# Attention queries of token tiles 2 and 3 made after the first head's scores, and three early heads instead of four

## The chip, the cores and the metric

The kernel runs on one core of a Trainium2 chip. Its engines work side by side, each through its own queue in program order: TensorE (PE, matrix products; PEld is its loading of weights), VectorE (DVE), ScalarE (ACT), GpSimdE (POOL) and SyncE (SP, which only issues transfers). They meet through semaphores. DMA engines move data between the chip's memory and the core's local memory. The metric is the device time of one execution in microseconds.

## The reference

One step of one decoder layer, for 512 prompt tokens and 32 sample tokens (8 sequences of 4), D = 1024, all in float32:

```
n = RMSNorm(h)
[u | conv input | q (4 heads x 128) | gates (3 x 1024)] = n @ w_in + b_in
branch A: S5 state space scan on u, GLU, projection
branch B: GLU, causal depthwise convolution (31 taps), LayerNorm, swish, projection
branch C: cross-attention of q into 256 memory tokens (4 heads), projection
h = h + (sum of sigmoid(gate_b) * branch_b) @ w_out
h = h + PEER(RMSNorm(h))
y = RMSNorm(h)
```

PEER, for each token: 8 heads; a head's query (256 wide) is scored against 2 x 128 keys, the best 16 of each half are combined and the best 16 of the 256 sums name 16 of 16384 experts. For each of the 128 experts chosen, a row u and a row v (1024 each) are fetched from a table: gelu(u . x) times the softmax of the scores weighs v, and the weighted rows are added to h.

## The kernel before

The tokens are cut into tiles of 128: tiles 0 and 1 are the first half (FIRST = 256 columns), tiles 2 and 3 and the 32 sample tokens (tile 4) the rest. The program has two parts.

**The trunk of the first half.** TensorE makes, in the order of the list JOBS, keys and values of the memory, the inputs of the three branches, the scan's products, the attention of tiles 0 and 1 and of the samples, gates and projections for 256 columns, and the output product (jobs o0 to o7). Each job is written into one of four pairs of PSUM banks, a pair is reused four jobs later, and weights come through a ring of six places of 512 KB (`load`). The attention queries are jobs q0 to q3: each is made by `weighted` for all 544 columns, as two halves of 272 columns over 8 slices of weights. In the profile a float32 product is two instructions, so a query is 32 of them; ScalarE adds the bias and writes qT.

**The experts.** An expert step n is one tile and one head; there are 34 steps (EXPERTS), and 16 rows each, so 544 rows. For each row POOL issues an indirect DMA that fetches u and v for 128 tokens (1 MB) into a ring of 10 places (RING). DVE takes the dot product with u, ScalarE applies gelu to four dots together, DVE multiplies by the softmax gate (`weigh`), and for three rows of four ScalarE builds a diagonal matrix with which TensorE adds the weighted v (line 1157); the fourth is added by DVE. Only then is the row's ring place free and POOL can fetch the row that is 10 later.

Between the two parts stands the routing. PEER queries of head 0 (Aq0) are made between the jobs o5 to o7; then TensorE runs the scores of head 0 (As0, line 1000), transposes of h (ht, L1006) and of the normalised input (xt, L1011), the queries of heads 1 and 2, the scores of head 1, and so on up to the scores of head EARLY_HEADS - 1. Queries and scores use four single PSUM banks in the order of BANK_JOBS. DVE routes head 0 (`route_first`; its indices let POOL fetch rows 0 to 15), then head 1 (`route(1)`), and after that begins with the dots; later routes are cut into pieces that run between dots. What is left, that is the heads from EARLY_HEADS on and the whole trunk of the second half (its attention, gates, projections, output product, norm, routing scores), is woven by `rest_of_trunk` into the expert rows: after each row TensorE takes 2 or 5 matrix products of it (`late_matmuls`). PLACE gives for each piece the row at which it falls, from its count in BANK_JOBS; ScalarE and DVE do their parts of it a few rows later. The weights of all this come through four places of 512 KB: `late_load` m waits until the product that used load m - 4 is done.

ScalarE's queue between the parts is: head 0's scores, h and x copies, then per early head the queries, the scores and, after some of them, the exponential of a routed head (`exp_of`), and only then gelu of the first dots.

Of the kernel before, what the change touches and what calls it, by code (L numbers as in the profile page):

```python
# [52 lines left out]
DIAGS = 8  # L53
LAG = 2
GROUP = 4
EARLY_HEADS = 4


COLS, _at = {}, 0
# [29 lines left out]

BANK_JOBS = [("As0.0", 0), ("Aq1.0", 0), ("As0.1", 0), ("Aq1.1", 0)]
for _h in range(1, PH):
    _late = int(_h >= EARLY_HEADS)
    if _h + 1 < PH:
# [107 lines left out]
def hybrid_step(nc, a, o):  # L203
    ctx = ExitStack()
    with ctx:
        def sem(name):
            return ctx.enter_context(nc.semaphore(name))
# [10 lines left out]
        def at(start, *shape):  # L218
            n = 1
            for x in shape:  # L220
                n *= x
            piece, first = (arenas[0], 0) if start < SPLIT_AT else (arenas[1], SPLIT_AT)
            v = piece[:, start - first:start - first + n]
            names = "abcd"[:len(shape)]
            if len(shape) > 1:
                v = v.rearrange(f"p ({' '.join(names)}) -> p {' '.join(names)}",
                                **{x: s for x, s in zip(names[1:], shape[1:])})
            return v
# [73 lines left out]
        h2sq = at(30976, KD, FIRST)  # L302
        xbT = at(44728, KD, FIRST)
        late_w = at(0, 4, 1024)
        qbuf = at(4096, 2, 2, RQ)
        gsg_b = at(22912, 2, 3, REST)
        merged_b = at(44728, KD, REST)
# [54 lines left out]
        def c(name, i=0, n=1):  # L362
# [37 lines left out]
        bank_full = [sem(f"bank_full{i}") for i in range(4)]  # L400
        bank_free = [sem(f"bank_free{i}") for i in range(4)]
        late_in = [sem(f"late_w_in{i}") for i in range(4)]
        x2b_in, mergeb_ok, h2sqb_ok, h2rb_ok, xbTb_ok = (sem(n) for n in (
            "x2b_in", "mergeb_ok", "h2sqb_ok", "h2rb_ok", "xbTb_ok"))

# [5 lines left out]
        def filled(eng, name):  # L411

            p, n = JOB[name]
            eng.wait_ge(full[p], n + 1)
            return pairs[p]
# [52 lines left out]
        def _(sp):  # L468
# [59 lines left out]
            def late_load(name, src, k=KD):  # L528
# [7 lines left out]
                    bank_filled(sp, BANK_LOADS[m - 4])  # L536
                sp.dma_start(late_w[:, m % 4, 0:k * P], src).then_inc(late_in[m % 4], 16)

            for h in range(PH):
                for b in range(2):  # L540
                    late_load(f"Aq{h}.{b}", a["peer_q"][2 * h + b])
# [27 lines left out]
        def _(pool):  # L569
# [58 lines left out]
            for g in range(TOPK * NJ):  # L628
                n, j = g // TOPK, g % TOPK
                if g == 0:  # L630
                    pool.wait_ge(half_routed, 1)
                elif g == 8:
                    pool.wait_ge(routed, 1)
                elif j == 0:
                    pool.wait_ge(routed, n + 1)
                if g == 6:
                    for t in range(2):
                        filled(pool, f"ht{t}")
                if g >= RING:
                    by, count = V_USERS[g - RING]  # L640
                    pool.wait_ge(v_used[by], count)
                    pool.sem_inc(slot_free, 1)
                pool.indirect_dma_start(row(g), None, a["peer_uv"],  # L643
                                        bass.IndirectOffsetOnAxis(ap=idx[:, n % 8, j:j + 1], axis=0)
                                        ).then_inc(row_in[g % RING], 16)
# [3 lines left out]
        def _(pe):  # L649
# [116 lines left out]
                mm.then_inc(full[JOB[f"z1{h}"][0]], 1)  # L766
            weighted("ai3", nT)
            for j in range(4):
                weighted(f"q{j}", nT)
            gates(0, 1)  # L770

            for n in ("q0", "q1", "q2", "q3", "k0", "k1", "k2", "k3", "v"):
# [230 lines left out]
            for t in range(2):  # L1003
                ps = flat(begin(f"ht{t}"), 1024)
                for k in range(KD):
                    mm = pe.transpose(ps[:, k * P:(k + 1) * P], h2T[:, k, t * P:(t + 1) * P], ident)  # L1006
                mm.then_inc(full[JOB[f"ht{t}"][0]], 1)
            for t in range(2):
                ps = flat(begin(f"xt{t}"), 1024)
                for k in range(KD):  # L1010
                    mm = pe.transpose(ps[:, k * P:(k + 1) * P], xbT[:, k, t * P:(t + 1) * P], ident)  # L1011
                mm.then_inc(full[JOB[f"xt{t}"][0]], 1)
            pe.wait_ge(rcol_ok, 1)
            for _ in first_queries(1):
                pass
            for _ in first_heads(1, EARLY_HEADS):
# [23 lines left out]
            def late_attention(t, stage):  # L1040

                for b in range(2):
                    name = f"b{stage}{t}.{b}"
                    ps = begin_bank(name)
                    if stage == "a":
                        pe.wait_ge(kv_copied, 48)
                    elif stage == "t":
                        pe.wait_ge(bp_ok, 2 * (t - 2) + b + 1)
                    else:
                        bank_emptied(pe, f"bt{t}.{b}")  # L1050
                    share = shares_b(b)
                    for h in range(2):
                        if stage == "a":
                            mm = pe.matmul(ps[:, MEM * h:MEM * (h + 1)], qT[:, 2 * b + h, t * P:(t + 1) * P],
                                           kT_b[:, 2 * b + h, :], start=True, stop=True)
                            if h == 1:
                                mm.then_inc(bank_full[BANK[name][0]], 1)
                            yield
                            continue
                        for m in range(2):  # L1060
                            part = share[:, h, P * m:P * (m + 1)]
                            if stage == "t":
                                n = 2 * h + m
                                mm = pe.transpose(ps[:, P * n:P * (n + 1)], part, ident)
                            else:
                                mm = pe.matmul(ps[:, P * h:P * (h + 1)], values_b(m, 2 * b + h), part,
                                               start=(m == 0), stop=(m == 1))
                            if h == 1 and m == 1:
                                mm.then_inc(bank_full[BANK[name][0]], 1)
                            yield  # L1070
# [95 lines left out]
        def _(act):  # L1166
# [86 lines left out]
            glu_input(3)  # L1253
            for j in range(4):
                ps = filled(act, f"q{j}")
                act.activation(halves(qT[:, j, :]), two(ps), ACT.Identity, bias=c("b_in", 12 + j)
                               ).then_inc(drained(f"q{j}"), 1)
            act.wait_ge(q_zero, 1)
            for j in range(4):
# [138 lines left out]
            for t in range(2):  # L1398
                ps = filled(act, f"ht{t}")
                act.wait_ge(kv_copied, 48)  # L1400
                act.activation(h2(t), flat(ps, 1024), ACT.Copy).then_inc(drained(f"ht{t}"), 1)
            for t in range(2):
                ps = filled(act, f"xt{t}")
                act.activation(xb(t), flat(ps, 1024), ACT.Copy).then_inc(drained(f"xt{t}"), 1)
            first_query(1)
            for h in range(1, EARLY_HEADS):
                first_query(h + 1)
                if h == 1:
                    act.wait_ge(rcol_ok, 3)
                first_score(h)  # L1410
                if h != 2:
                    exp_of(h // 2)

            def late_exps(t, b):

# [931 lines left out]
```

## Time and profile before

| | us |
|---|---|
| median of 3 runs | 1943.35 (1941.68 to 1944.21) |
| profiled execution | 1947.41 |
| its span, first to last instruction | 1945.6 |
| PE / DVE / ACT / POOL busy | 1674.4 / 1388.4 / 521.7 / 663.9 |
| mean granted TensorE clock | 0.949 |

Durations below are of the profiled execution, in microseconds from the start of its span unless marked otherwise. A granted clock of 1.00 is 2.4 GHz and 0.50 is 1.2 GHz. DMA share is the mean busy share of the 16 DMA engines. A line number is that of the code or of a helper. An entry in square brackets gives the engine's idle time before the instruction and what ended it.

### The profile page before, as it was taken

The numbers are of one execution on the slowest core, as the hardware profiler recorded it, in microseconds if no ns is written. First come the engines' busy times: TensorE is split into PE (matmuls) and PEld (weight loads), VectorE is DVE, ScalarE is ACT, GpSimd is POOL, SyncE is SP. The second block draws the span as 40 slices with busy tenths as digits, with TensorE's granted clock in tenths as the row PEclk, the third lists the DMA queues.
The fourth block names the chain that finished last, engine by engine and source line by source line (L and its number), as shares of the span: only waits on it lengthen the run. The fifth ranks groups of instructions, "written<-read, shape, count | busy, mean of one in ns | idle before, by whom it ended". The sixth has DMA issues, their size and how long they took to land.

```text
span 1945.6 us, 17733 instructions
## 1 busy us (share of the span) xinstructions
PE 1674.4 (86%) x5411; PEld 999.5 (51%) x5411; DVE 1388.4 (71%) x3407; ACT 521.7 (27%) x1203; POOL 663.9 (34%) x605
## 2 busy tenths in 40 slices
PE   8999999999888999998868999877777777787876
PEld 7888987887555555554434555323333212333332
DVE  5998684227788777777787778776777776777754
ACT  3121142113333433332222223332222122321221
POOL 0020030002434343333434344444444453445441
PEclk9999999999999999999979999998999898989898
DMA  5452465548999999999989999999999999999995
GB/s 209 141 87 98 154 146 164 176 150 339 418 400 412 419 418 418 418 419 401 419 349 413 419 420 414 421 422 410 414 419 413 412 416 419 408 414 415 421 412 245
DMA packets 112687, 675.14 MB, mean 347 GB/s; under 512 B 12784, under 2 KB 15296, under 8 KB 42576
## 3 DMA queue, kind: packets, MB, share of 16 engines
q0 software_dynamic: 80816, 577.23, 73.0%
q1 hardware_dynamic: 31216, 95.87, 14.3%
q10 hardware_dynamic: 560, 0.92, 0.2%
q8 instruction: 43, 0.70, 0.1%
q14 instruction: 52, 0.43, 0.1%
HBM read 665.79 MB, written 6.21 MB: 345 GB/s over the span
## 4 chain that ended last, share of the span: by engine, by line
PE 46%; DMA 36%; issue 8%; DVE 6%; POOL 2%; ACT 2%; ACTq 0%; DVEq 0%; POOLq 0%
DMA upper<-in_peer_uv,upper 20%; PE pair L1157 19%; DMA lower<-in_peer_uv,upper 16%; PE pair L667 7%; PE pair L678 6%; PE pair L1024 4%; DVE upper L2080 2%; PE pair L781 2%; ACT upper L1550 1%; PE pair L972 1%; POOL upper L643 1%; DVE lower L2080 1%; POOL lower L643 1%; PE pair L793 1%; PE pair L712 1%
## 5 line engine op out<-in xcount | busy, mean ns | idle before, releaser
L1157 PE MATMUL pair<-upper 128*128 128x512 f32 (+1 forms) x1144 | 570.4, 641 | 152.6 <-ACT upper L1550 152.3
L643 POOL DMA_INDIRECT upper<-in_peer_uv,upper x324 | 369.2, 1139 | 500.6 <-PE pair L1157 437.4
L1157 PE MATMUL pair<-lower,upper 128*128 128x512 f32 (+1 forms) x772 | 382.1, 637 | 93.7 <-ACT upper L1550 93.6
L1157 PEld LDWEIGHTS pair<-upper 128*128 128x128 f32 (+1 forms) x1144 | 218.5, 198 | 434.0 <-issue 276.0
L643 POOL DMA_INDIRECT lower<-in_peer_uv,upper x220 | 255.2, 1160 | 483.0 <-PE pair L1157 305.0
L2080 DVE CUSTOM_DVE_ANT_0 upper<-upper 128x1024 f32<-128x1024 f32 x172 | 210.7, 1225 | 122.4 <-DMA upper<-in_peer_uv,upper 122.1
L1157 PEld LDWEIGHTS pair<-lower,upper 128*128 128x128 f32 (+1 forms) x772 | 148.0, 198 | 283.5 <-issue 185.5
L2080 DVE CUSTOM_DVE_ANT_0 upper<-upper,lower 128x1024 f32<-128x1024 f32 x152 | 185.8, 1222 | 87.6 <-DMA upper<-in_peer_uv,upper 86.7
L1550 ACT ACTIVATE upper<-upper 128x128 f32<-128x128 f32 (+1 forms) x479 | 159.9, 386 | 308.3 <-DVE upper L2096 308.1
L2080 DVE CUSTOM_DVE_ANT_0 lower<-lower,upper 128x1024 f32<-128x1024 f32 x116 | 142.1, 1225 | 85.5 <-DMA lower<-in_peer_uv,upper 85.5
L1024 PE MATMUL pair<-lower 128*128 128x288 f32 x704 | 194.0, 413 | 2.6 <-ACT upper L1420 2.6
L1367 ACT ACTIVATE upper<-upper 128x4 f32<-128x4 f32 (+1 forms) x139 | 34.4, 247 | 595.9 <-DVE upper L2080 595.8
L1024 PEld LDWEIGHTS pair<-lower 128*128 128x128 f32 x704 | 135.8, 194 | 78.2 <-issue 51.8
L2080 DVE CUSTOM_DVE_ANT_0 lower<-lower 128x1024 f32<-128x1024 f32 x104 | 127.0, 1222 | 52.6 <-DMA lower<-in_peer_uv,upper 52.0
L667 PE MATMUL pair<-lower 128*128 128x272 f32 x576 | 133.1, 393 | 1.8 <-ACT lower L1237 1.8
L667 PEld LDWEIGHTS pair<-lower 128*128 128x128 f32 x576 | 109.5, 190 | 24.6 <-issue 2.5
L1752 DVE SCALAR_TENSOR_TENSOR upper<-upper 128x512 f32<-128x512 f32 x120 | 80.3, 747 | 0.0
L1367 ACT ACT_TABLE_LOAD x57 | 73.1, 1283 | 1.0
L678 PE MATMUL pair<-lower 128*128 128x256 f32 x320 | 71.6, 380 | 0.0
L1024 PE MATMUL pair<-upper,lower 128*128 128x288 f32 x256 | 69.6, 407 | 0.9 <-DVE upper L2150 0.9
L678 PEld LDWEIGHTS pair<-lower 128*128 128x128 f32 x320 | 60.5, 190 | 7.9
L1024 PEld LDWEIGHTS pair<-upper,lower 128*128 128x128 f32 x256 | 48.8, 191 | 27.6 <-issue 16.0
(420 smaller groups left out, 1760.6 us busy)
## 6 DMA issues: line engine op xcount, KB each, us to landing
lower<-in_w_in SPq DMA_DIRECT2D x64, 512.0 KB, 7.0
lower<-in_peer_q SPq DMA_DIRECT2D x32, 512.0 KB, 7.9
lower<-in_proj SPq DMA_DIRECT2D x48, 256.0 KB, 7.1
lower<-in_w_out SPq DMA_DIRECT2D x16, 512.0 KB, 6.0
upper<-in_peer_uv,upper POOLq DMA_INDIRECT x324, 11.8
upper<-in_cache_k SPq DMA_DIRECT2D x8, 512.0 KB, 4.5
upper<-in_cache_v SPq DMA_DIRECT2D x8, 512.0 KB, 3.7
lower<-in_peer_uv,upper POOLq DMA_INDIRECT x220, 11.8
```

The costliest lines, as they stand in the source:

```text
L643: pool.indirect_dma_start(row(g), None, a["peer_uv"], bass.IndirectOffsetOnAxis(ap=idx[:, n % 8, j:j + 1], axis=0)).then_inc(row_in[g % RI ...
L667: mm = pe.matmul(ps[:, h, 0:HT], w[:, j, :], rhs[:, j, h * HT:(h + 1) * HT], start=(j == 0), stop=(j == k - 1))
L678: mm = pe.matmul(one_bank(ps), w[:, j, :], rhs[:, j, 0:FIRST], start=(j == 0), stop=(j == k - 1))
L712: mm = pe.matmul(ps[:, 0, 0:MEM], w[:, k, :], memT[:, k, :], start=(k == 0), stop=(k == KD - 1))
L781: mm = pe.matmul(one_bank(ps), w[:, j, :], nT[:, j, 0:FIRST], start=(j == 0), stop=(j == KD - 1))
L793: mm = pe.matmul(ps[:, 0, 0:MEM], masked_q[:, HEADS * b + h, :], kc[:, h, :], start=(b == 0 and h == 0), stop=(b == NB - 1 and h == HEADS ...
L1024: mm = pe.matmul(ps[:, 0:REST], w[:, j, :], x[:, j, :], start=(j == 0), stop=(j == k - 1))
L1157: mm = pe.matmul(pairs[n % 2][0:rows, h, :], diag[:, (nth - 1) % DIAGS, 0:rows], row(g)[:, D + h * 512:D + (h + 1) * 512], start=(j == min ...
L1367: act.activation(gel[:, n % 2, lo:hi], dots[:, n % 2, lo:hi], ACT.Gelu, scale=rcol[:, t:t + 1] if t < 2 else 1.0).then_inc(gel_ok, 1)
L1550: act.activation(diag[:, nth % DIAGS, 0:cols], turn, ACT.Copy, scale=weight[:, n % 8, j:j + 1]).then_inc(diag_ok, 1)
L1752: stt(v, tail, w, v, ALU.mult, ALU.add).then_inc(conv_step, 1)
L2080: dve.tensor_tensor_reduce(u, u, xb(EXPERTS[n][0]), 1.0, 0.0, ALU.mult, ALU.add, dots[:, n % 2, j:j + 1]).then_inc(u_used, 1)
```

## The change

Jobs q0 to q3 are made for the first 256 columns and the 32 sample columns only, each slice of weights with a product of 256 and one of 32 columns. The 256 columns of tiles 2 and 3 are four new products mq0 to mq3, two ahead of the transposes of x and two behind them, each 8 products of 256 columns. Their weights are loaded a second time, by four loads of 512 KB, into the places of ring rows 8 and 9, and POOL fetches row 8 only after mq1 and row 9 only after mq3. ScalarE copies the four results into qT. EARLY_HEADS is 3 instead of 4, so the queries of head 4 and the scores of head 3 become the first woven pieces. The late attention scores wait until the copies of mq are done.

```diff
-EARLY_HEADS = 4
+EARLY_HEADS = 3
-BANK_JOBS = [("As0.0", 0), ("Aq1.0", 0), ("As0.1", 0), ("Aq1.1", 0)]
+BANK_JOBS = [("As0.0", 0), ("mq0", 0), ("As0.1", 0), ("mq1", 0), ("mq2", 0), ("mq3", 0), ("Aq1.0", 0), ("Aq1.1", 0)]
...
+        kept_w = at(33024, HALF, 1024)
...
+            sp.wait_ge(lnx_ok, 2 * HALF - 1)
+            for j in range(HALF):
+                sp.dma_start(kept_w[:, j, :], a["w_in"][12 + j]).then_inc(kept_in[j], 16)
             for h in range(PH):
                 for b in range(2):
                     late_load(f"Aq{h}.{b}", a["peer_q"][2 * h + b])
...
+                if g in (8, 9):
+                    bank_filled(pool, f"mq{2 * g - 15}")
...
             for j in range(4):
-                weighted(f"q{j}", nT)
+                w = loaded(f"q{j}")
+                ps = begin(f"q{j}")
+                for k in range(KD):
+                    pe.matmul(ps[:, 0, 0:FIRST], w[:, k, :], nT[:, k, 0:FIRST], start=(k == 0), stop=(k == KD - 1))
+                    mm = pe.matmul(ps[:, 1, 0:NB * NT], w[:, k, :], nT[:, k, SEQ:], start=(k == 0), stop=(k == KD - 1))
+                mm.then_inc(full[JOB[f"q{j}"][0]], 1)
...
+            def middle_queries(lo, hi):
+                for j in range(lo, hi):
+                    pe.wait_ge(kept_in[j], 16)
+                    ps = begin_bank(f"mq{j}")
+                    for k in range(KD):
+                        mm = pe.matmul(ps[:, 0:SEQ - FIRST], kept_w[:, j, k * P:(k + 1) * P], nT[:, k, FIRST:SEQ],
+                                       start=(k == 0), stop=(k == KD - 1))
+                    mm.then_inc(bank_full[BANK[f"mq{j}"][0]], 1)
+            pe.wait_ge(rcol_ok, 1)
+            middle_queries(0, 2)
             for t in range(2):
                 ps = flat(begin(f"xt{t}"), 1024)
...
-            pe.wait_ge(rcol_ok, 1)
+            middle_queries(2, 4)
             for _ in first_queries(1):
                 pass
...
                     if stage == "a":
                         pe.wait_ge(kv_copied, 48)
+                        for h in range(2):
+                            bank_emptied(pe, f"mq{2 * b + h}")
...
-                act.activation(halves(qT[:, j, :]), two(ps), ACT.Identity, bias=c("b_in", 12 + j)
+                act.activation(qT[:, j, 0:FIRST], ps[:, 0, 0:FIRST], ACT.Identity, bias=c("b_in", 12 + j))
+                act.activation(qT[:, j, SEQ:], ps[:, 1, 0:NB * NT], ACT.Identity, bias=c("b_in", 12 + j)
                                ).then_inc(drained(f"q{j}"), 1)
...
+            def middle_query(j):
+                ps = bank_filled(act, f"mq{j}")
+                act.activation(qT[:, j, FIRST:SEQ], ps[:, 0:SEQ - FIRST], ACT.Identity, bias=c("b_in", 12 + j)
+                               ).then_inc(bank_drained(f"mq{j}"), 1)
+            middle_query(0)
+            middle_query(1)
             for t in range(2):
                 ps = filled(act, f"xt{t}")
                 act.activation(xb(t), flat(ps, 1024), ACT.Copy).then_inc(drained(f"xt{t}"), 1)
+            middle_query(2)
+            middle_query(3)
             first_query(1)
             for h in range(1, EARLY_HEADS):
                 first_query(h + 1)
                 if h == 1:
                     act.wait_ge(rcol_ok, 3)
                 first_score(h)
-                if h != 2:
-                    exp_of(h // 2)
+                exp_of(h - 1)
```

## Rows read from the trace of the kernel before

**Rows 1.** The page, section 2: GB/s in 40 equal slices of the span.
```profile
GB/s 209 141 87 98 154 146 164 176 150 339 418 400 412 419 418 418 418 419 401 419 349 413 419 420 414 421 422 410 414 419 413 412 416 419 408 414 415 421 412 245
```

**Rows 2.** Windows: length, engines' busy time, then PEclk, DMA share, GB/s.
```profile
500.00:550.00 50.00, 42.58 (x154) 26.01 (x152) 39.46 (x94) 16.09 (x41) 20.77 (x20) 1.00 1.02 420
1000.00:1050.00 50.00, 35.77 (x111) 19.13 (x110) 42.53 (x101) 14.68 (x34) 20.30 (x18) 0.86 0.87 356
```

**Rows 3.** The chain of waits, 155 to 192: start, duration, what.
```profile
155.12 36.67 PE pair L667 x160
```

**Rows 4.** The chain of waits, 214 to 217: L781 has 256 columns, L843 and L845 have 72.
```profile
214.64 0.48 PE pair L781 x2
215.12 0.17 PE pair L845 x2
215.29 0.48 PE pair L781 x2
215.78 0.28 PE pair L843 x2
```

**Rows 5.** Windows, columns as in Rows 2: L781 mixed with L843 and L845; L843 and L845 alone.
```profile
214.00:226.00 12.00, 12.00 (x70) 11.39 (x69) 6.67 (x10) 5.27 (x12) 0.00 (x0) 1.00 0.73 259
230.00:235.00 5.00, 5.00 (x25) 4.91 (x25) 5.00 (x17) 0.00 (x0) 0.00 (x0) 0.58 0.00 0
```

**Rows 6.** Timeline of DVE, 150 to 345: start, duration, instruction, idle before.
```profile
214.40 1.23 DVE L1820 TENSOR_REDUCE upper<-pair 128x4 f32<-128x1024 f32 x1 [5.37 <-PE pair L819]
...
308.53 0.35 DVE L1890 TENSOR_SCALAR upper<-pair,upper 128x128 f32<-128x128 f32 x1 [10.27 <-PE pair L859]
```

**Rows 7.** Timeline of PE, 405 to 480: start, duration, instruction, idle before.
```profile
435.38 1.91 PE L1006 MATMUL pair<-upper 128*128 128x128 f32 x16
438.44 2.01 PE L1011 MATMUL pair<-upper 128*128 128x128 f32 x16 [1.15 <-ACT upper L1401]
440.29 13.98 PE L972 MATMUL pair<-upper,lower 128*128 128x256 f32 x64
...
469.70 1.05 PE L983 MATMUL pair<-upper,lower 128*128 128x128 f32 x8
474.06 3.75 PE L1157 MATMUL pair<-lower,upper 128*128 128x512 f32 x4 [3.31 <-ACT upper L1550]
```

**Rows 8.** Windows, columns as in Rows 2: weights arriving early on; beside job o2.
```profile
6.00:8.00 2.00, 1.76 (x4) 1.51 (x5) 0.00 (x0) 2.00 (x8) 0.00 (x0) 1.00 0.98 418
404.00:406.00 2.00, 2.00 (x11) 1.77 (x10) 0.00 (x0) 0.00 (x1) 0.00 (x0) 1.00 0.90 244
```

**Rows 9.** Timeline of DVE, 425 to 485.
```profile
456.06 0.49 DVE L1968 MAX8 upper<-lower 128x8 f32<-128x128 f32 x2 [9.39 <-ACT lower L1394]
...
465.38 1.22 DVE L2080 CUSTOM_DVE_ANT_0 lower<-lower 128x1024 f32<-128x1024 f32 x1
...
470.24 1.21 DVE L2080 CUSTOM_DVE_ANT_0 lower<-lower 128x1024 f32<-128x1024 f32 x1
```

**Rows 10.** Timeline of ACT, 405 to 485: gelu of the first four dots.
```profile
472.99 0.30 ACT L1367 ACTIVATE upper<-upper 128x4 f32<-128x4 f32 x1
```

**Rows 11.** Timeline of POOL, 405 to 485: issue of ring rows 9 and 10.
```profile
453.71 0.94 POOL L643 DMA_INDIRECT upper<-in_peer_uv,upper  x1 [0.30 <-issue]
478.63 0.93 POOL L643 DMA_INDIRECT lower<-in_peer_uv,upper  x1 [23.99 <-PE pair L1157]
```

**Rows 12.** Timeline of SP's queue, 432 to 475: late loads of 512 KB.
```profile
433.36 36.87 SPq L537 DMA_DIRECT2D lower<-in_peer_q  x10
```

**Rows 13.** Windows, columns as in Rows 2: where the ring's first fill ends.
```profile
478.00:488.00 10.00, 10.00 (x33) 6.68 (x32) 9.72 (x28) 1.28 (x4) 4.71 (x4) 0.90 0.90 312
```

**Rows 14.** Timeline of DVE, 1000 to 1014: the second half's norm, then row 12's dot.
```profile
1005.97 1.94 DVE L2162 RECIPROCAL upper<-upper 128x288 f32<-128x288 f32 x1
...
1012.83 1.22 DVE L2080 CUSTOM_DVE_ANT_0 upper<-upper,lower 128x1024 f32<-128x1024 f32 x1
```

**Rows 15.** Windows, columns as in Rows 2: behind the second half's norm.
```profile
1014.00:1024.00 10.00, 9.38 (x23) 4.22 (x24) 9.60 (x24) 3.86 (x10) 3.42 (x3) 0.74 0.31 111
```

More of the change, by code:

```diff
@@ L402, in hybrid_step @@
         late_in = [sem(f"late_w_in{i}") for i in range(4)]
+        kept_in = [sem(f"kept_w_in{i}") for i in range(HALF)]
         x2b_in, mergeb_ok, h2sqb_ok, h2rb_ok, xbTb_ok = (sem(n) for n in (
```

## The prediction

> **What bounds the kernel now.** Read the page's second section first. From the eleventh slice on (48.6 us each) the DMA engines move about 418 GB/s to the end; in the first nine they move 87 to 209 [rows 1]. In a window inside the expert rows their share is 1.02 at 420 GB/s while TensorE is busy for 42.6 of 50 and DVE for 39.5 [rows 2]. So the span has two parts with different limits. In the trunk TensorE works through its own queue without a break: the chain of waits names nothing but its products, as in the 36.67 us that hold two earlier products and the queries [rows 3]. In the expert part the limit is the bytes of 544 rows. Time in which the DMA engines stand dry there is lost for good, since the rows that remain need the same time whenever they start. The change acts where the two parts meet, so the third view is the timeline of each engine from 430 to 490. There the ring of ten rows is filled once: row 9 is issued at 453.71, row 10 only at 478.63, when TensorE has used up row 0 [rows 11]. Ten rows of 1.05 MB and the eight late loads of 0.52 MB issued beside them (ten in all, two of them sooner) [rows 12] are 14.7 MB, 35 us at 418 GB/s: the transfers run out just as row 10 is issued, and 478 to 488 shows 312 GB/s instead of 418, a loss of 2.5 us only [rows 13]. The cover is used up to its end, which decides this case.
>
> **The change, part by part.** Times that I call shifted are on the clock of the trace before; the trunk's gain is taken off at the end.
>
> *Trunk queries.* 160 instructions take 36.67, so 0.229 each; a query has 32, 7.33 us, and four have 29.3 [rows 3]. Now a slice of weights has two instructions of 256 columns and two of 32. The trace has no pair of this form; nearest is the pair of 256 beside a pair of 72, 0.48 + 0.17 or 0.48 + 0.28 [rows 4]. I take 0.65, since 32 columns are fewer than 72: a query 8 x 0.65 = 5.2, four 20.8, a gain of 8.5. Bounds: with 0.76, a gain of 5.0; with 32 columns at the column rate of the 256 (0.216 / 256 x 32 = 0.027 an instruction), 8 x (0.432 + 0.054) = 3.9 a query, a gain of 13.8. Does the gain pass on? DVE stood idle for 5.37 before the attention scores of tile 0 and for 10.27 before the sample values [rows 6]. The first wait shrinks to nothing, but its results are used only some 40 us later, and the second stays, because TensorE's products lead there. So the 8.5 arrive at o0 in full; if DVE led, they would be lost. ScalarE has two copies for one, in gaps.
>
> *Weights loaded twice.* Four loads, 2.1 MB, go out on SP behind o7's and ahead of Aq0's. In this stage 244 GB/s are moved, while weights came at 418 early on [rows 8]. They take 5 us, and Aq0's two loads, issued three and seven us later, are needed twelve us later: nothing. SP's new wait was over long before. If they came at 244 only, Aq0's second load would be late by 0 to 2.
>
> *Products moved.* Four times 16 instructions of 256 columns: the 64 of L972 take 13.98, 13.8 from start to next start [rows 7]. They begin when ht is done, and fill the stop ahead of xt (1.15, with the overlap of two groups 1.3). Everything behind, first Aq1, starts 13.8 - 1.3 = 12.5 later, shifted. POOL's waits cost nothing: mq1 is done at 444 and mq3 at 452.6, when row 8 and row 9 are due (452.5 and 453.7) [rows 11]; even a delay would vanish in the queue of 25 us of rows.
>
> *The dots wait.* DVE begins route(1) at 456.06, when ScalarE has copied head 1's scores, after 9.39 of idling; the first dot comes at 465.38, behind it in program order [rows 9]. Head 1's scores stand behind all four mq, so route(1) starts at 468.6, the first dot comes at 477.9, and the fourth, before at 470.24, ends at 484. One early head less helps ScalarE and TensorE but not this: before, gelu of these dots was held until 472.99 by ScalarE's work on head 3 [rows 10], and now that is gone but DVE is later still. DVE takes the fifth dot before it weighs, so TensorE's first row, before at 474.06 [rows 7], starts at about 486.2, and row 10 is issued 12.1 later. Bounds: 11 if all of gelu's hold is won back, 14 if TensorE, now idle for 11 instead of 3.31 (As3 ended at 470.75; 12.5 later less head 4's queries and head 3's scores, 7.8), stays longer at 1.2 GHz than before.
>
> *Transfers.* In that time they run dry, and what was put behind them is no cover. Worse, the loads of head 6 were released by head 4's queries, in the first fill; now these are woven pieces behind row 10. Two loads, 1.05 MB, move from covered time to saturated time: 2.5 at 418. Bounds: 0, if they fit into the gap of 478 to 488, and 2.5.
>
> *Woven pieces.* Head 4's queries (16) and head 3's scores (4) come in front: 20 steps at 11 in four rows, so all that follows falls 7 rows later. Its products were made before too; TensorE's rows have room for them. The routes still find their scores: those of the second half's first head are copied at row 220, wanted at 224. One place matters. The second half's norm holds DVE from 1005.97 to 1012.83 [rows 14], right after the eleventh dot counted from 0 in a step, with four dots unweighed; behind it the transfers move 111 GB/s for 10 us, 7.3 lost [rows 15]. Seven rows later the block falls behind dot 2: there the rows before are released, which is one row more of cover (2.5), but two dots instead of one follow until the next weighing (1.2 and some routing). I take a gain of 1.0, with bounds from a gain of 7.3 to a loss of 2.
>
> Sum: -8.5 + 12.1 + 2.5 - 1.0 = +5.1. The profiled execution took 1947.41, 1.8 more than its span of 1945.6 and 4.06 more than the median; I carry the difference to the median: 1943.35 + 5.1 = 1948.5.
>
> One rule speaks for another sum. The Trainium skill, page "TensorE: Matmul & The Clock Gate", section "Back-to-back issue gap", gives a product of up to 64 columns as about 60 cycles, 25 ns warm, when taken alone. By it, as an estimate, the 32 columns would cost next to nothing and the four queries would gain 13.9. The trace does not bear it out for instructions that each load their weights: 72 columns take 85 to 140 ns [rows 4].
>
> **Rivals.**
> 1. *The narrow products are free.* The gain is 13.8, the sum -0.2: 1943.2. For it: the weights' load could lie under the product of 256. Against: beside the same 256, narrow pairs showed 0.17 and 0.28 [rows 4].
> 2. *The norm's stop goes (the other side).* Place: the expert row of the norm of the second half. If the seven rows shift it to where the rows issued cover it, the 7.3 come back: -8.5 + 12.1 + 2.5 - 7.3 = -1.2, 1942.2. It decides once the rows in flight at its start last longer than DVE's 6.9, the dots to the next weighing and a landing of some 10. For it: the stop is an accident of a step's phase. Against: only one row of cover is gained.
> 3. *The clock falls in the query stage.* Alone, the 72 columns ran at 0.58 of the clock, mixed with 256 at 1.00 [rows 5]. If half of the 20.8 ran at 1.2 GHz, it would add 10.4: 1958.9.
> 4. *The trunk's gain is covered by another engine.* Then it is +13.6: 1957.0. Against: DVE's idle times [rows 6].
> 5. *The rows are not bound by transfers, the delay is absorbed.* Only the gain is left: 1934.9. Against: a share of 1.02 wherever no stop is seen [rows 2].
>
> **How the numbers follow.** My forecast 0.63 (its own range 1945.0 to 1952.0), rivals 0.05, 0.15, 0.06, 0.04 and 0.07. A measurement of this kernel can tell about 0.2%, 3.9 us, from no change: below 1939.5 lie rival 5 and a little of rival 2, 0.09; between 1939.5 and 1947.2 the rest of rivals 1 and 2 and nearly a fourth of my own case, 0.34; above 1947.2 the rest, 0.57. From 1941.0 to 1955.0 all but 0.19 is held: above it lie rivals 3 and 4, below it rival 5 and a fringe of rival 2.
>
> **What would show it.** In the changed kernel: queries q0 to q3 five to six us apart on ScalarE, at clock 1.00; the first row fetched about 8.5 earlier; head 1's scores copied, and route(1) started, about 4 later; first row on TensorE near 477.7; between the first fill and row 10's fetch a dry stretch of about 12 us in the DMA windows, where now there is none; after it 418 GB/s as before. I am wrong if row 10 is fetched before 479, or if the rows after it take less time than before.

## The result and the profile after

The changed kernel takes 1953.0 (median of five runs, 1951.21 to 1954.05) against 1944.21 for the kernel before on the same chip: a ratio of 1.0043, 95% interval 1.0029 to 1.0056. It is slower by 8.8, where +5.1 was forecast. The direction held, and so did the range with the rivals in it, 1941.0 to 1955.0; the forecast's own range, 1945.0 to 1952.0, ends 1.0 below the measurement.

The profiled execution has a span of 1951.1. The page's section 2 answers to [rows 1]; its slices are now 48.8 long:

```profile
GB/s 209 140 87 120 156 158 188 165 159 286 416 397 366 419 418 418 418 418 414 420 387 381 421 419 420 412 422 422 419 412 411 421 416 412 417 418 419 414 407 265
```

Two places differ from before. The tenth slice has fallen from 339 to 286: that is the restart of the rows. The thirteenth (585 to 634) has fallen from 412 to 366: a new stop, which the prediction did not have. The dip of the second half's norm, 349 in one slice before, is spread over two, 387 and 381.

**Trunk.** The chain of waits in the query stage (start, duration, what; columns 256 in L779 and 32 in L780), and ScalarE's timeline with the four queries:

```profile
163.74 0.14 PE pair L780 x2
163.88 0.51 PE pair L779 x2
```
```profile
168.50 0.47 ACT L1282 ACTIVATE upper<-pair,upper 128x256 f32<-128x256 f32 x1 [4.14 <-PE pair L780]
173.74 0.47 ACT L1282 ACTIVATE upper<-pair,upper 128x256 f32<-128x256 f32 x1 [4.59 <-PE pair L780]
...
184.22 0.47 ACT L1282 ACTIVATE upper<-pair,upper 128x256 f32<-128x256 f32 x1 [4.59 <-PE pair L780]
```

A slice of weights takes 0.14 + 0.51 = 0.65, and the queries come 5.24 apart, against 7.33 before [rows 3]. The granted clock of this stage was 1.00.

**Restart.** TensorE, DVE, ScalarE and POOL between 427 and 484 answer to [rows 7, 9, 10 and 11]:

```profile
427.49 1.91 PE L1018 MATMUL pair<-upper 128*128 128x128 f32 x16
429.24 7.07 PE L1026 MATMUL pair<-lower,upper 128*128 128x256 f32 x32
436.15 1.91 PE L1035 MATMUL pair<-upper 128*128 128x128 f32 x16
437.90 7.07 PE L1026 MATMUL pair<-lower,upper 128*128 128x256 f32 x32
444.81 13.98 PE L984 MATMUL pair<-upper,lower 128*128 128x256 f32 x64
...
478.16 3.75 PE L1183 MATMUL pair<-lower,upper 128*128 128x512 f32 x4 [10.68 <-ACT upper L1586]
```
```profile
460.57 0.49 DVE L2004 MAX8 upper<-lower 128x8 f32<-128x128 f32 x2 [21.80 <-ACT lower L1421]
...
469.88 1.22 DVE L2116 CUSTOM_DVE_ANT_0 lower<-lower 128x1024 f32<-128x1024 f32 x1
```
```profile
476.00 0.30 ACT L1394 ACTIVATE upper<-upper 128x4 f32<-128x4 f32 x1 [6.30 <-DVE upper L2116]
```
```profile
434.53 1.00 POOL L650 DMA_INDIRECT lower<-in_peer_uv,upper  x1 [133.69 <-DVE upper L2105]
...
445.81 0.94 POOL L650 DMA_INDIRECT upper<-in_peer_uv,upper  x1 [0.30 <-issue]
482.72 0.94 POOL L650 DMA_INDIRECT lower<-in_peer_uv,upper  x1 [35.97 <-PE pair L1183]
```

The first row is fetched at 434.53, 7.90 sooner than before, but row 10 at 482.72, 4.09 later: 12.0 more lie between them, which is what the products mq do alone (below). In the windows (length, busy PE, PEld, DVE, ACT, POOL, then clock, DMA share, GB/s) the transfers stand still meanwhile; the third line is the new stop of the thirteenth slice:

```profile
470.00:484.00 14.00, 5.84 (x12) 2.99 (x13) 13.85 (x41) 1.28 (x4) 0.94 (x1) 0.63 0.02 7
...
500.00:550.00 50.00, 41.29 (x136) 25.22 (x135) 37.30 (x92) 15.74 (x42) 18.40 (x17) 0.93 1.01 420
596.00:608.00 12.00, 12.00 (x36) 6.86 (x35) 6.92 (x18) 3.06 (x6) 4.35 (x4) 0.92 0.57 205
```

**The new stop.** Between 585 and 600 TensorE reaches g0.0, the first gate product of the second half (L1048), while ScalarE makes the late exponentials of tile 3 (L1456):

```profile
588.41 1.05 PE L995 MATMUL pair<-upper,lower 128*128 128x128 f32 x8
593.89 1.64 PE L1048 MATMUL pair<-lower 128*128 128x288 f32 x4 [4.43 <-ACT upper L1456]
595.32 3.19 PE L1183 MATMUL pair<-lower,upper 128*128 128x512 f32 x4
```
```profile
586.60 0.30 ACT L1394 ACTIVATE upper<-upper 128x4 f32<-128x4 f32 x1 [3.77 <-DVE upper L2116]
589.41 0.69 ACT L1586 ACTIVATE upper<-upper 128x128 f32<-128x128 f32 x2 [2.50 <-DVE upper L2132]
...
591.43 1.28 ACT L1456 ACT_TABLE_LOAD   x1
592.73 0.47 ACT L1456 ACTIVATE upper<-pair,upper 128x256 f32<-128x256 f32 x1
```
```profile
590.40 0.94 POOL L650 DMA_INDIRECT upper<-in_peer_uv,upper  x1 [0.30 <-issue]
599.32 1.53 POOL L650 DMA_INDIRECT lower<-in_peer_uv,upper  x1 [7.98 <-PE pair L1183]
```

The diagonals for rows 40 and 41 (L1586) are ready at 590, but their products (L1183) stand behind g0.0 in TensorE's queue. g0.0 needs the PSUM bank that the exponential of ba3.0, the attention scores of tile 3, empties, and ScalarE makes that in row 42, behind those diagonals. So POOL gets no free place for 8.0. In the kernel before the same wait was 2.18:

```profile
565.01 2.02 PE L1024 MATMUL pair<-lower 128*128 128x288 f32 x4 [2.18 <-ACT upper L1420]
```

### The profile page after: what moved, and what is told of

It is laid out like the page before. It is cut to its first block, busy times and chain, and to the rows that moved or that the text cites. A ratio compares the mean times of both kernels' runs of the same rounds, so it can differ in the third digit from the quotient of the medians.

```text
span 1951.1 us, 17882 instructions
## 1 busy us (share of the span) xinstructions
PE 1675.8 (86%) x5475; PEld 1004.1 (51%) x5475; DVE 1388.1 (71%) x3407; ACT 523.8 (27%) x1211; POOL 662.4 (34%) x605
## 4 chain that ended last, share of the span: by engine, by line
PE 44%; DMA 35%; DVE 8%; issue 8%; ACT 2%; POOL 2%; ACTq 0%; DVEq 0%; POOLq 0%; SPq 0%
DMA upper<-in_peer_uv,upper 19%; PE pair L1183 18%; DMA lower<-in_peer_uv,upper 16%; PE pair L685 6%; PE pair L674 5%; PE pair L1048 4%; DVE upper L2116 2%; PE pair L793 2%; PE pair L984 1%; DVE lower L2116 1%; ACT upper L1586 1%; POOL upper L650 1%; POOL lower L650 1%; PE pair L779 1%; PE pair L719 1%
## 5 line engine op out<-in xcount | busy, mean ns | idle before, releaser
L1183 PE MATMUL pair<-upper 128*128 128x512 f32 (+1 forms) x1144 | 569.3, 639 | 140.5 <-ACT upper L1586 140.5
L1183 PE MATMUL pair<-lower,upper 128*128 128x512 f32 (+1 forms) x772 | 382.5, 636 | 107.6 <-ACT upper L1586 107.6
L1183 PEld LDWEIGHTS pair<-upper 128*128 128x128 f32 (+1 forms) x1144 | 217.4, 198 | 418.4 <-issue 278.1
L1183 PEld LDWEIGHTS pair<-lower,upper 128*128 128x128 f32 (+1 forms) x772 | 147.1, 197 | 295.0 <-issue 204.5
L1586 ACT ACTIVATE upper<-upper 128x128 f32<-128x128 f32 (+1 forms) x479 | 160.3, 386 | 296.0 <-DVE upper L2132 295.8
L1048 PE MATMUL pair<-lower 128*128 128x288 f32 x704 | 189.7, 407 | 4.4 <-ACT upper L1456 4.4
L1048 PEld LDWEIGHTS pair<-lower 128*128 128x128 f32 x704 | 133.8, 191 | 76.1 <-issue 49.6
L674 PE MATMUL pair<-lower 128*128 128x272 f32 x448 | 103.8, 393 | 1.3 <-ACT lower L1263 1.3
L674 PEld LDWEIGHTS pair<-lower 128*128 128x128 f32 x448 | 85.0, 190 | 19.3 <-issue 2.0
L1048 PE MATMUL pair<-upper,lower 128*128 128x288 f32 x256 | 69.4, 406 | 0.0
L685 PEld LDWEIGHTS pair<-lower 128*128 128x128 f32 x320 | 60.3, 190 | 8.0
L1048 PEld LDWEIGHTS pair<-upper,lower 128*128 128x128 f32 x256 | 48.7, 190 | 26.5 <-issue 16.7
```

The costliest lines, as they stand in the source:

```text
L674: mm = pe.matmul(ps[:, h, 0:HT], w[:, j, :], rhs[:, j, h * HT:(h + 1) * HT], start=(j == 0), stop=(j == k - 1))
L685: mm = pe.matmul(one_bank(ps), w[:, j, :], rhs[:, j, 0:FIRST], start=(j == 0), stop=(j == k - 1))
L1048: mm = pe.matmul(ps[:, 0:REST], w[:, j, :], x[:, j, :], start=(j == 0), stop=(j == k - 1))
L1183: mm = pe.matmul(pairs[n % 2][0:rows, h, :], diag[:, (nth - 1) % DIAGS, 0:rows], row(g)[:, D + h * 512:D + (h + 1) * 512], start=(j == min ...
L1586: act.activation(diag[:, nth % DIAGS, 0:cols], turn, ACT.Copy, scale=weight[:, n % 8, j:j + 1]).then_inc(diag_ok, 1)
```

## The experiments

A ratio is to the kernel before, timed beside each, with its 95% interval. A dry stretch below is the loss against 418 GB/s, summed over windows of 2 us from 500 on that show less than 330. Times and ratios come from all executions; rows, waits and dry stretches come from the one that was profiled. That one can lie some us from its kernel's median (1944.3 against 1950.2 with the shift alone, 1956.1 against 1950.2 with the gap of two, 1953.9 against 1949.2 with the gap of six). So a trace shows where a wait arises and where it goes, and only the ratios show what it costs.

**Each part alone.** First the narrow trunk queries alone, from the kernel before:

```diff
-                weighted(f"q{j}", nT)
...
+                    pe.matmul(ps[:, 0, 0:FIRST], w[:, k, :], nT[:, k, 0:FIRST], start=(k == 0), stop=(k == KD - 1))
+                    mm = pe.matmul(ps[:, 1, 0:NB * NT], w[:, k, :], nT[:, k, SEQ:], start=(k == 0), stop=(k == KD - 1))
...
+                act.activation(qT[:, j, FIRST:SEQ], nT[:, j, FIRST:SEQ], ACT.Copy)
```

> The kernel before with the narrow trunk queries alone (256 and 32 columns). The queries of tiles 2 and 3 are left out: their place in qT is filled with a copy of other data in ScalarE's idle time. Four early heads, no second load of weights. Transfer theory (the rows are bound by transfers and everything ahead of the first row counts in full): the first row is fetched 8.4 earlier (four queries of 5.24 instead of 7.33) and the end is 8.4 earlier, about 1936 against 1944, ratio 0.9957. Absorption theory (later stops of the rows swallow what happens at their start): ratio above 0.9985. Covered-gain theory (DVE leads in the trunk): the first row is fetched less than 4 earlier.

Measured 0.9959 (0.9947 to 0.9972). The gain of 8.0 reaches the end in full; the first row is fetched 7.7 sooner. Then the products mq alone, with the trunk's queries whole and four early heads (their weights, waits and copies as in the change):

```diff
+            pe.wait_ge(rcol_ok, 1)
+            middle_queries(0, 2)
...
-            pe.wait_ge(rcol_ok, 1)
+            middle_queries(2, 4)
```

> The kernel before with the four products mq at the new place alone: the trunk makes all queries as before, the weights are loaded a second time, and mq makes those of tiles 2 and 3 once more. Four early heads. Transfer theory: head 1's scores, route(1) and the first dot come 12.5 later, row 10 is fetched 12 to 12.5 later after a dry stretch of about 10, the loads of head 6 stay in the first fill, and the end is 12.5 later: about 1956.5, ratio 1.0064. Absorption theory: under 1.002. If the second load of weights disturbs Aq0's, the first row too is later, by up to 2.

Measured 1.0059 (1.0047 to 1.0072): 11.5 slower, with row 10 fetched 12.05 later. Both sizes are as forecast. Then three early heads alone:

```diff
-EARLY_HEADS = 4
+EARLY_HEADS = 3
...
-                if h != 2:
-                    exp_of(h // 2)
+                exp_of(h - 1)
```

> The kernel before with three early heads instead of four, nothing else. Transfer theory: gelu of the first dots is no longer held by head 3 on ScalarE, row 10 is fetched 1 to 1.5 earlier; two loads (1.05 MB, 2.5 at 418 GB/s) move from the first fill to the saturated time; the woven pieces fall 7 rows later (-1, uncertain by 3): together +0.3, between -2 and +3, ratio 1.000. Place theory (the seven rows are what costs, by stops that DVE's late pieces make): ratio 1.002 or more, with the first rows unchanged and the loss collecting between rows 16 and 270.

Measured 1.0040 (1.0027 to 1.0053). My theory expected next to nothing of this part (+0.3), and it costs 7.8. Row 10 comes 1.0 sooner, and the loss appears later. Last, the shift without the work: four early heads and 20 empty steps of the woven work.

```diff
+    if _h == EARLY_HEADS:
+        BANK_JOBS += [("gapx", 20)]
...
+                for _ in range(20):
+                    yield
```

> The kernel before with 20 empty steps in front of the woven pieces, so that all of them fall 7 rows later while the early heads, their loads and the start of the rows stay. Transfer theory: the stop at the second half's norm becomes shorter by about 1, the rest is unchanged: -1, between -3 and +2, ratio 0.9995. Place theory: it carries the loss that the changed kernel shows beyond its first rows (about 3): ratio 1.0015 or more.

Measured 1.0034 (1.0021 to 1.0047): 6.6 of the 7.8 come with the shift alone. The loads of head 6, which this kernel doesn't move, would be the other 1.2; the two intervals don't tell that from nothing or from my 2.5.

**The change with four early heads.**

```diff
-EARLY_HEADS = 3
+EARLY_HEADS = 4
...
-                exp_of(h - 1)
+                if h != 2:
+                    exp_of(h // 2)
```

> The changed kernel with four early heads again: head 3's scores are made ahead of the rows, with its two loads ahead of them, and no woven piece is shifted by seven rows. My theory after the first four runs: the sum of the two parts measured alone, -8.4 (narrow queries on the trunk) and +11.0 (query products ahead of the rows), so about +2.6, ratio 1.0013 (1.0005 to 1.0025); row 10 fetched about 4.4 later than before, and no dry stretch of the transfers of over 3 us between rows 16 and 60. Rival: the parts don't add, the three heads are not what costs; then about 1.0043 as the whole change.

Measured 1.0016 (1.0005 to 1.0027), row 10 fetched 2.2 later where 4.4 was expected (in this execution the first row was already 2.3 sooner than in the change's; from it to row 10 are 48.6, as against 48.2), and a dry stretch of 1.5 at 594 to 602. The two parts add, and going from four early heads to three is what the change loses beyond them.

**The products behind the scores.** ScalarE's copies of mq2 and mq3 fall in row 2 here.

```diff
-            pe.wait_ge(rcol_ok, 1)
-            middle_queries(0, 2)
...
-            middle_queries(2, 4)
+            pe.wait_ge(rcol_ok, 1)
...
             for _ in first_heads(1, EARLY_HEADS):
                 pass
+            middle_queries(0, 4)
```

> The changed kernel with the eight narrow query products moved behind all three early heads' scores on TensorE (As0, Aq1, Aq2, As1, As2 and then mq0 to mq3), and their evictions behind the early heads' exponentials on ScalarE; still three early heads. Theory: what lengthens the restart of the rows is the order, not the number of products: row 10 would be fetched at most 1 later than before against the shifted start of the rows, that is about 7 earlier than before on the span's clock, and the time would be -8.4 + 0.5 + (4 to 7 for the shifted pieces and the moved loads): -4 to -1, ratio 0.998 to 0.9995. Rival: the products cost TensorE's time wherever they stand before the first row's matmul, since that row waits for TensorE; then 1.003 to 1.0045, as the whole change.

Measured 0.9989 (0.9980 to 0.9998). In POOL's timeline row 10 is fetched 8.8 sooner than before [rows 11]:

```profile
469.81 1.59 POOL L652 DMA_INDIRECT lower<-in_peer_uv,upper  x1 [0.41 <-issue]
```

The same 64 instructions, run while DVE routes, put 0.7 between the first row and row 10 (36.9, against 36.2 before); ahead of the scores they put 12 there. They are not free even so: rows 8 and 9, whose places the weights hold, come 18 and 23 later than at the pace of rows 0 to 7, and 460 to 470 shows 228 GB/s, a loss of 4.5. The stop at 586 to 600 stays, 7.8.

**The steps made up early.**

```diff
-    return 5 if j % 4 == 3 else 2
+    return (5 if j % 4 == 3 else 2) + int(g < 40 and g % 2 == 0)
```

> The changed kernel with one more woven matmul on every other of the first 40 rows, so that the 20 steps of head 3's scores are made up early and all later pieces fall at the rows at which they fall before the change. If the place of tile 3's pieces against the rows is what costs (about 6 of the 8.8), the dry stretch at 596 to 608 us goes and the time is +3 to +5, ratio 1.0015 to 1.0026. If it is that head 3 and its loads are in the rows at all, whatever their place, or the restart alone, it stays at 1.004 or more.

Measured 1.0052 (1.0040 to 1.0064): my theory of the place of a piece in its expert step fell. g0.0 ends in row 35 as before the change, and yet TensorE waits 7.47 for the late exponential and the dry stretch is 8.7:

```profile
581.90 1.30 PE L1048 MATMUL pair<-lower 128*128 128x288 f32 x2 [7.47 <-ACT upper L1456]
```
```profile
576.95 0.30 ACT L1394 ACTIVATE upper<-upper 128x4 f32<-128x4 f32 x1 [0.55 <-DVE upper L2116]
579.03 0.40 ACT L1586 ACTIVATE upper<-upper 128x128 f32<-128x128 f32 x1 [1.78 <-DVE upper L2132]
579.45 1.28 ACT L1456 ACT_TABLE_LOAD   x1
580.74 0.47 ACT L1456 ACTIVATE upper<-pair,upper 128x256 f32<-128x256 f32 x1
```

This led to the theory that held. It is not the row that counts but whether g0.0 starts in the same group of four rows as its exponential. ScalarE does a row's piece behind the gelu of its group and the row's own diagonal, and these wait for DVE: gelu for the four dots, the diagonals for `weigh`. TensorE needs the diagonals too, for the products of the group's rows. If g0.0 lies in the same group, TensorE therefore comes to it only when gelu is past. If the exponential lies in the next group, TensorE comes too early, and stands in front of g0.0 until ScalarE has got through that part of the next group. How much of it falls into the wait differs: here TensorE is free at 574.4, and gelu (576.95), `weigh`, the diagonal, a table load of 1.28 and the exponential all follow; in the change gelu (586.60) was just over when TensorE came at 589.46, and the 4.43 are ScalarE's own work behind it.

**A gap ahead of g0.0.**

```diff
+BANK_JOBS += [("gapg", 6)]
...
+                for _ in range(6):
+                    yield
```

> The changed kernel with six idle steps of the woven work on TensorE ahead of g0.0, the first gate product of the second half, so that it starts in row 42 and not in row 39. Theory: TensorE, in order, stands before g0.0 until ScalarE has made the late exponential ba3.0, which it makes in row 42, behind the gelu of rows 40 to 43; a start in row 39 therefore holds up the matmuls of rows 40 to 42 (4.4 to 7.5 us of wait in the four kernels so far in which it lies across that gelu, 2.2 where it doesn't). With the gap the wait goes below 2.5, the dry stretch at 596 to 608 us loses about 5, and the time falls from 1.0043 to 1.0010 to 1.0025. Rival: the three heads cost by their own work and loads, wherever the pieces stand; then 1.0038 to 1.0050.

Measured 1.0023 (1.0011 to 1.0034), 0.20% less than the change, with an uncertainty of 0.18 on the difference. There is no wait at g0.0 any more and no dry stretch at 585 to 612; the windows show 419 and 415 there:

```profile
590.00:600.00 10.00, 6.62 (x18) 3.17 (x17) 9.61 (x23) 6.51 (x18) 3.35 (x3) 0.83 1.01 419
600.00:612.00 12.00, 12.00 (x40) 7.21 (x39) 10.89 (x31) 5.03 (x10) 5.98 (x5) 1.00 1.02 415
```

With two steps instead of six:

> The same gap with two idle steps: g0.0 starts in row 40, two rows before its exponential but in the same group of four rows, as before the change (row 32 against 35). If the boundary of the group decides, the wait is about 2.2 as before the change and the time within 0.1% of that with six steps; if only the distance in rows decides, the wait stays at 4 or more and the time at about 1.004.

Measured 1.0028 (1.0014 to 1.0041), and the wait is that of before, although the exponential is still two rows behind:

```profile
597.16 1.55 PE L1049 MATMUL pair<-lower 128*128 128x288 f32 x4 [2.04 <-ACT upper L1459]
```

The wait speaks for the group's boundary; the time alone would not settle it, since its interval reaches near that of the change. And with six steps where the products stand behind the scores:

> The kernel with the query products behind all early scores, and the gap of six steps. Without the gap it measured 0.9989 and had a dry stretch of 7.8 us at 586 to 600 us. Theory: the gap gives back about 5: ratio 0.9955 to 0.9975. Rival (the stop has another cause): 0.998 to 0.9998 as without the gap.

Measured 0.9979 (0.9968 to 0.9989): 0.10% faster than without the gap, where 0.14 to 0.34 was expected, with an uncertainty of 0.14 on the difference. The dry stretch of 7.8 at 586 to 600 is gone, but 2.7 appear at 642 to 650, and the largest stop, at the second half's norm, goes from 4.2 to 6.0. TensorE shows a wait of 4.4 at 636 (at 648 in the kernel with the gap of six) that the same kernels without the gap don't have. A gap moves everything behind it too.

Over all kernels, with g0.0's first row on TensorE and the row of the exponential ba3.0 worked out from the counts of the pieces; "dry there" is summed over the 25 us around and behind g0.0's start:

| kernel | g0.0, exponential | same group | longest wait at g0.0 | dry there |
|---|---|---|---|---|
| before | 32, 35 | yes | 2.18 | 2.7 (two stretches) |
| narrow trunk queries alone | 32, 35 | yes | 2.18 | 1.3 |
| products mq alone | 32, 35 | yes | 2.18 | 1.5 |
| change with four heads | 32, 35 | yes | 2.2 | 1.0 |
| gap of two | 40, 42 | yes | 2.04 | 2.6 |
| gap of six | 42, 42 | yes | none | none |
| products behind scores, gap of six | 42, 42 | yes | none | none |
| products woven, gap of eight (below) | 44, 44 | yes | 0.44 | none |
| change | 39, 42 | no | 4.43 | 6.0 |
| three heads alone | 39, 42 | no | 5.81 | 6.5 |
| shift alone | 39, 42 | no | 7.43 | 4.0 |
| products behind scores | 39, 42 | no | 5.7 | 7.8 |
| steps made up early | 33, 36 | no | 7.47 | 8.7 |
| products woven (below) | 42, 44 | no | 3.68 | 1.1 |

**A second place of the same kind.** No run was aimed at it, but the traces show it: bt2.0, the first transpose of tile 2's late attention (L1090), needs the bank that ScalarE's copy of Aq6.0 (L1413) empties. Before, it starts in row 16 and the copy lies in row 17, in the same group, and TensorE does not wait. In the change it starts in row 23 and the copy lies in row 24, behind the next group's gelu. The kernel before, then the change on TensorE and on ScalarE:

```profile
520.99 0.38 PE L1064 MATMUL pair<-upper 128*128 128x128 f32 x2
```
```profile
541.86 1.05 PE L995 MATMUL pair<-upper,lower 128*128 128x128 f32 x8
547.21 0.69 PE L1090 MATMUL pair<-upper 128*128 128x128 f32 x2 [4.30 <-ACT lower L1413]
```
```profile
544.48 0.30 ACT L1394 ACTIVATE upper<-upper 128x4 f32<-128x4 f32 x1 [6.66 <-DVE upper L2116]
546.49 0.40 ACT L1586 ACTIVATE upper<-upper 128x128 f32<-128x128 f32 x1 [1.71 <-DVE upper L2132]
546.79 0.64 ACT L1413 ACTIVATE lower<-pair 128x256 f32<-128x256 f32 x2
```

All seven kernels in which it is 23 and 24 (the change, three heads alone, the shift alone, the products behind the scores, and the three of these with a gap of two or six) wait 4.30 to 5.05 here and show a dry stretch of 1.9 to 4.3 between 540 and 560. With the steps made up early (19 and 20, also across) the wait is 1.95 and nothing runs dry; the four kernels with 16 and 17 and the two woven ones (27 and 27) show neither. A gap ahead of g0.0 leaves this place as it is, so what the gap does not give back is not the three heads' own work alone.

**The products woven between the rows.**

```diff
-    return 5 if j % 4 == 3 else 2
+    return 5 if j % 4 == 3 else 3 if j % 8 == 1 else 2
...
+                    for j in range(HALF if h == 5 else 0):
+                        late_load(f"mq{j}", a["w_in"][12 + j])
...
+                        for j in range(HALF):
+                            yield from middle_query(j)
```

> The kernel before with the narrow queries on the trunk and the query products of tiles 2 and 3 woven between the rows, as late pieces behind head 4's scores, their weights loaded late through the ring as the others are; four early heads, no kept places. Theory: nothing ahead of the rows is lengthened, 2.1 MB more are loaded while the transfers are saturated: 2.1 MB at 418 GB/s is 5.0; -8.4 + 5.0 = -3.4, ratio 0.9983, and up to 1.0005 if the woven pieces fall at places that stop the engines as they did in the run with the shift alone. Rival: more woven pieces always stop the rows; then over 1.001.

Measured 0.9958 (0.9944 to 0.9973), median 1936.7: ahead of both kernels. The first two lines of the edit make room for the 32 new steps: TensorE takes two more woven products for every 16 rows. No run has this faster pace alone, so what part it has in the gain is open. Row 10 is fetched 9.1 sooner than before. The 5.0 that I gave the 2.1 MB did not show in the time, to within 3.7. In the traces the dry stretches and lesser losses from 500 to 1900 add up to 12.5 against 16.6 with the trunk's part alone, and row 10 to the last row takes 1437.4 against 1436.5: 0.9 more, which is 5.0 less the 4.1. So the bytes may have cost what I gave them, and smaller losses paid for it; why these are smaller was not tested. With a gap of eight steps as well:

> The kernel with the query products woven between the rows, four early heads, and a gap of eight steps ahead of g0.0, so that it starts in row 44 (row 42 without it, across the gelu from the exponential of row 44; wait 3.7, dry stretch 1.1). Theory: little is lost there, so little comes back: 0 to -2 against 0.9958, that is 0.9948 to 0.9960. Rival: the wait of 3.7 passes in full; then 0.994.

Measured 0.9964 (0.9951 to 0.9976), no gain that could be told. The wait falls to 0.4 and row 64 is fetched 2.3 sooner than without the gap, but by row 272 it is 2.8 later.

## Why the prediction was right, and where it was wrong

**Trunk queries: right.** Forecast 5.2 a query and -8.5; measured 5.24, -7.90 at the first row, and -8.0 alone at the end. The pair of 72 columns was a good neighbour: 0.65 a slice was forecast and measured. The estimate by the Trainium skill ("TensorE: Matmul & The Clock Gate", section "Back-to-back issue gap"), -13.9 from its figure for a product taken alone, does not hold for products that each load their weights: 64 of 256 columns took 13.98 [rows 7], two of them 0.437, so two of 32 add 0.22 to a slice, 0.11 each.

**Weights loaded twice: right.** Forecast nothing; in the run with the products alone the first row is fetched at 442.34, against 442.43 before.

**Restart: right.** Forecast against measured on the new clock: route(1) 460.1 and 460.57, first dot 469.4 and 469.88, first row on TensorE 477.7 and 478.16, row 10 at 482.2 and 482.72. From ht to Aq1 the delay is 17.32 - 4.91 = 12.4 (12.5 forecast). The transfers lost 13.8 from 470 to 484 and 1.0 in the two us after, less the 2.5 of before [rows 13]: 12.2 in all. The run with the products alone put 11.5 on it.

**Head 6's loads: open.** Forecast +2.5; the runs bound it no better than 1.2 with an uncertainty of about 3.5.

**Woven pieces: the step that failed.** "One place matters", the prediction said, and priced the second half's norm at -1.0. The dry stretches around the norm were 1.3 and 7.2 before, and are 2.9 and 4.5 after, 1.1 less; but the three other kernels with nothing shifted show 6.7 to 7.3 there in all, no more than the change's 7.4, so this gain can't be told from none. What the prediction did not have is the other places. The rows moved seven places, not a multiple of four, and pairs of woven pieces on two engines came to lie across a gelu. At g0.0 and ba3.0 this took a wait of 2.18 to 4.43 and the dry stretches from 2.7 to 6.0; at bt2.0 and the copy of Aq6.0 it made a wait of 4.30 and a dry stretch of 1.9 where there was none. Together that is +5.2 in the two traces. The whole term measured +6.6 alone, where -1.0 was forecast. So the term's sign was wrong, and it makes up more than the difference between +5.1 and +8.8. That the waits come from the groups is shown by the runs; how much time each place costs is less sure. The gap returned 0.20% of the change's 0.43%, near 4, with an uncertainty of 0.18%; behind the scores it returned 0.10%, with one of 0.14%. I had the waits of before at this place in the trace and did not ask what makes them short.

The parts add to -0.41 + 0.59 + 0.40 = +0.58%, against 0.43% measured whole; with some 0.13 of uncertainty on each, that agrees.

Of the signs named ahead, "after it 418 GB/s as before" failed in the thirteenth slice; the others came, and row 10 to the last row takes 1440.4 against 1437.1, not less. No rival came: the narrow products were not free, the norm's stop did not go, the clock of the query stage stayed at 1.00, the trunk's gain passed on, and the delay of the rows was not absorbed.

## What to carry to other kernels

Where two engines run woven work by a count, and one of them does its share behind a step that closes a group, price a shift by the group: see for each pair of pieces whether producer and consumer stay on the same side of that step. Work that must stand between two phases belongs where the next phase's longest engine is already busy: the same products put 12 ahead of row 10 when they stood before the scores that DVE waited for, and 0.7 behind them, where only the ring places held for their weights cost the transfers 4.5. And before work is moved out of a saturated stretch to a place ahead of it, price it inside: woven between the rows, at a pace raised for it, it came out cheapest.

## What was not expected of the hardware

The woven products with 2.1 MB of weights beside saturated transfers were as fast as the kernel that leaves that work out (0.9958 and 0.9959, to within 0.19%). That does not show bytes that cost nothing: in the traces the other losses are smaller by 4.1 (12.5 against 16.6), about what the bytes should cost, and why they are smaller is open.
